# A one-core trunk kernel: stick-breaking attention outputs computed channel-major by column tiles, their norm moved

## The reference, cut to what matters

```python
z = einsum("bqhd,bkhd->bhqk", q_i, k_p) * scale
w = exp(where(past, z + suffix, -inf))     # suffix: sums of log sigmoid(-z)
outs.append(einsum("bhqk,bkhd->bqhd", w, v_p))
...
sb_o = rms_norm(stick_breaking_attention(q, k, v), sb_gain)   # over each head's 64 channels
```

## Time and profile before

| | us |
|---|---|
| median of 3 runs | 1591.11 |
| lowest, highest | 1590.86, 1613.55 |
| profiled execution | 1608.1 |
| its span | 1606.4 |

### The profile page before, as it was taken

The page is one execution under the profiler, slowest core; times in us unless marked ns, Lnnn a source line. Parts: engine busy times, 40 slices in busy tenths (PEclk is TensorE's granted clock), DMA queues, the critical chain, the costliest instruction groups (busy, mean ns, idle before and its releaser), DMA issues.

```text
span 1606.4 us, 22550 instructions
## 1 busy us (share of the span) xinstructions
PE 1535.4 (96%) x8129; PEld 1294.0 (81%) x8129; DVE 700.9 (44%) x1283; ACT 479.2 (30%) x1089; POOL 529.0 (33%) x478
## 2 busy tenths in 40 slices
PE   5999999999987999999999999999999999999997
PEld 4778888888867888888887888888888888888885
DVE  5105546455443567666224143334333443344337
ACT  5223444454342334443344211111111111111114
POOL 3112332333233446654342323323323332332331
PEclk8999999999995899989999999999999999999999
DMA  5112222332232122221521211111111111111112
GB/s 171 41 52 68 84 67 81 115 91 79 65 108 77 48 79 64 63 79 52 195 80 50 69 53 52 40 52 52 46 45 52 40 51 52 52 39 52 52 40 104
DMA packets 144602, 110.61 MB, mean 69 GB/s; under 512 B 5568, under 2 KB 132112, under 8 KB 144528
## 3 DMA queue, kind: packets, MB, share of 16 engines
q1 hardware_dynamic: 144384, 109.11, 22.6%
q10 hardware_dynamic: 144, 0.52, 0.1%
HBM read 88.63 MB, written 20.99 MB: 68 GB/s over the span
## 4 chain that ended last, share of the span: by engine, by line
PE 91%; DVE 6%; issue 1%; ACT 1%; POOL 1%; DMA 0%; DVEq 0%; SPq 0%; POOLq 0%
PE banks L1738 10%; PE banks L1740 10%; PE banks L1739 10%; PE banks L259 9%; PE banks L261 9%; PE banks L260 9%; PE banks L1777 5%; PE banks L1778 5%; PE banks L1776 5%; PE banks L947 3%; PE banks L961 3%; PE banks L644 2%; PE banks L996 2%; PE banks L954 1%; PE banks L621 1%; DVE area L1841 1%
## 5 line engine op out<-in xcount | busy, mean ns | idle before, releaser
L251 POOL TENSOR_TENSOR w_l<-w_raw,w_h 128x1024 fp32r<-128x1024 f32 x113 | 274.7, 2431 | 645.1 <-ACT w_h L1785 345.9
L1738 PE MATMUL banks<-act_h,w_h 128*128 128x512 f32 x704 | 275.0, 391 | 2.4 <-DVE act_l L310 2.4
L1740 PE MATMUL banks<-act_h,w_l 128*128 128x512 f32 x704 | 274.5, 390 | 0.0
L1739 PE MATMUL banks<-act_l,w_h 128*128 128x512 f32 x704 | 274.5, 390 | 0.0
L259 PE MATMUL banks<-act_h,w_h 128*128 128x512 f32 x624 | 251.1, 402 | 8.0 <-POOL w_l L251 5.5
L261 PE MATMUL banks<-act_h,w_l 128*128 128x512 f32 x624 | 245.2, 393 | 0.0
L260 PE MATMUL banks<-act_l,w_h 128*128 128x512 f32 x624 | 244.6, 392 | 0.0
L1841 DVE TENSOR_TENSOR area<-area,banks 128x512 f32<-128x512 f32 x352 | 237.4, 687 | 0.0
L1835 DVE TENSOR_TENSOR area<-banks,area 128x512 f32<-128x512 f32 x44 | 30.4, 692 | 443.3 <-PE banks L1740 442.5
L1738 PEld LDWEIGHTS banks<-act_h,w_h 128*128 128x128 f32 x704 | 132.5, 188 | 30.0 <-DVE act_l L310 2.6
L1740 PEld LDWEIGHTS banks<-act_h,w_l 128*128 128x128 f32 x704 | 132.6, 188 | 27.6
(11 more groups left out here) (192 smaller groups left out, 2040.3 us busy)
## 6 DMA issues: line engine op xcount, KB each, us to landing
w_raw<-in_w_in SPq DMA_DIRECT2D x31, 512.0 KB, 4.0
w_raw<-in_w_gate SPq DMA_DIRECT2D x22, 512.0 KB, 3.8
w_raw<-in_w_up SPq DMA_DIRECT2D x22, 512.0 KB, 3.8
w_raw<-in_w_down SPq DMA_DIRECT2D x22, 512.0 KB, 3.5
area<-in_x SPq DMA_DIRECT2D x8, 1024.0 KB, 9.2
projected_tm<-area SPq DMA_DIRECT2D x32, 256.0 KB, 2.9
w_raw<-in_w_out SPq DMA_DIRECT2D x16, 512.0 KB, 3.6
projected_cm<-area SPq DMA_DIRECT2D x20, 256.0 KB, 2.2
```

The source lines that it names most:

```text
L251: e.tensor_tensor(w_l[:, b], w_raw[:, b], w_h[:, b].bitcast(F32), ALU.subtract).then_inc(sems["wl_ready"], 1)
L1738: e.matmul(dst, w_h[:, b, k], act_h[:, k, cols], start=(k == 0), stop=False)
L1739: e.matmul(dst, w_h[:, b, k], act_l[:, k, cols], start=False, stop=False)
L1740: mm = e.matmul(dst, w_l[:, b, k], act_h[:, k, cols], start=False, stop=(k == KT - 1))
```

## The change

- **Values.** `weigh` swaps the operands: the 64 channels of v are stationary, the 128 tokens of `wt` move, so that the output has channels on the partitions. Head 0 goes to PSUM partitions 0-63, head 1 to 64-127 of the same columns: two column tiles of the PE array. Both units of a pair are weighed together, in odd slots, the heads in turns.
- **Store.** The output goes to its own DRAM tensor `attended`, [2, 128 channels, 1024 tokens]; `projected_tm` loses its last 256 columns. The squares on ACT and their waits are gone.
- **Norm.** In the mixer's step t = -1 four pieces (head pair x 512 tokens) are loaded into `gate`, squared on ACT, summed per head over the partitions by a PE matmul with a block matrix of ones, Ln and Exp on ACT, times gain on DVE, split into `act_h` (ACT) and `act_l` (DVE). SP issues piece i's load after piece i - 1's product (`so_done`).
- **Mixer.** `final_sb` is gone, `mix` has 768 channels, the second `mix_turn` has 2 transposes instead of 4 and waits for `fin_hg` alone, the first for `fin_dn`. `gates` and the first output product wait for the pieces. Constants grow by one memset and two selects on POOL.

```diff
-    TM = SB_AT + SBW
+    TM = SB_AT
...
+    sb_dram = nc.dram_tensor("attended", [2, P, T], F32, kind="Internal").ap()
...
+            m = head_ones[:, :].rearrange("p (b r) -> p b r", r=64)
+            select(m, ALU.is_ge, 0, [[-64, 2], [0, 64]], 1, 0.0)
+            select(m, ALU.is_ge, 63, [[64, 2], [0, 64]], -1, 0.0)
...
-                e.dma_start(tm_dram[q * P:(q + 1) * P, SB_AT + hp * P:SB_AT + (hp + 1) * P],
-                            o_stage[:, u % 2]).then_inc(sems[f"o_stored{u % 2}"], 16)
+                e.dma_start(sb_dram[hp, :, q * P:(q + 1) * P], o_stage[:, u % 2]).then_inc(sems[f"o_stored{u % 2}"], 16)
...
-                reach(e, "wt_ready", k + 1)
-                if hh == 0 and at == 0:
+                e.wait_ge(sems["wt_ready"], k + 2)
+                if at == 0:
                     reach(e, "o_evac", u)
                 for j in range(n // P):
                     m = NT - 1 - q + at // P + j
-                    mm = e.matmul(Ov[:, u % 2, hh, :], wt[:, k % 2, j * P:(j + 1) * P],
-                                  v_tm[:, m, hp * P + hh * SBD:hp * P + (hh + 1) * SBD],
-                                  start=(hh == 0 and at == 0 and j == 0), stop=(at + (j + 1) * P == (q + 1) * P), skip_group_check=True)
-                mm.then_inc(sems["av_done"], 1)
+                    for hh in range(2):
+                        mm = e.matmul(O[hh * SBD:(hh + 1) * SBD, u % 2 * P:(u % 2 + 1) * P],
+                                      v_tm[:, m, hp * P + hh * SBD:hp * P + (hh + 1) * SBD], wt[:, (k + hh) % 2, j * P:(j + 1) * P],
+                                      start=(at == 0 and j == 0), stop=(at + (j + 1) * P == (q + 1) * P), skip_group_check=True)
+                        if j == n // P - 1:
+                            mm.then_inc(sems["av_done"], 1)
...
-                if 2 <= k < NH + 2:
-                    weigh(k - 2)
+                if 3 <= k < NH + 2 and k % 2 == 1:
+                    weigh(k - 3)
...
-            def out_squares(k):
-                hp, q = UNITS[k][:2]
-                u = unit_of(k)
-                reach(e, "o_evac", u + 1)
-                reach(e, "o_sq", u)
-                for hh in range(2):
-                    ins = e.activation(junk_o[:, hh, :], o_stage[:, u % 2, hh * SBD:(hh + 1) * SBD], ACT.Square,
-                                       accum_out=ssq_sb[:, q, 2 * hp + hh:2 * hp + hh + 1])
-                ins.then_inc(sems["o_sq"], 1)
...
+        def piece(i):
+            return i // 2, slice(i % 2 * HALF, (i % 2 + 1) * HALF)
+
+        def attended_sync(e, i):
+            hp, cols = piece(i)
+            reach(e, "so_done", i)
+            e.dma_start(gate[:, 0:HALF], sb_dram[hp, :, cols]).then_inc(sems["so_loaded"], 16)
+
+        def attended_sums(e, i):
+            e.wait_ge(sems["so_sq"], i + 1)
+            reach(e, "so_ln", i)
+            e.matmul(bank(4), head_ones[:, :], junk_dn[:, :, :], start=True, stop=True).then_inc(sems["so_sum"], 1)
+
+        def attended_squares(e, i):
+            e.wait_ge(sems["so_loaded"], 16 * (i + 1))
+            reach(e, "so_sum", i)
+            e.activation(junk_dn[:, :, :], heads(gate[:, 0:HALF]), ACT.Square).then_inc(sems["so_sq"], 1)
+
+        def attended_length(e, i):
+            e.wait_ge(sems["so_sum"], i + 1)
+            reach(e, "so_low", i)
+            e.activation(mix[:, 0:HALF], bank(4), ACT.Ln, scale=1.0 / SBD, bias=eps_col[:, 0:1]).then_inc(sems["so_ln"], 1)
+            e.wait_ge(sems["so_ln"], i + 1)
+            e.activation(mix[:, 0:HALF], mix[:, 0:HALF], ACT.Exp, scale=-0.5).then_inc(sems["so_r"], 1)
+
+        def attended_high(e, i):
+            hp, cols = piece(i)
+            e.wait_ge(sems["so_done"], i + 1)
+            e.activation(act_h[:, hp, cols], mix[:, 0:HALF], ACT.Copy).then_inc(sems["so_high"], 1)
+
+        def attended_done(e, i):
+            e.wait_ge(sems["so_r"], i + 1)
+            e.wait_ge(sems["gain_col_loaded"], 32)
+            e.scalar_tensor_tensor(out=mix[:, 0:HALF], in0=gate[:, 0:HALF], scalar=gain_col[:, 0:1], in1=mix[:, 0:HALF],
+                                   op0=ALU.mult, op1=ALU.mult).then_inc(sems["so_done"], 1)
+
+        def attended_low(e, i):
+            hp, cols = piece(i)
+            e.wait_ge(sems["so_high"], i + 1)
+            e.wait_ge(sems["so_done"], i + 1)
+            e.tensor_tensor(act_l[:, hp, cols], mix[:, 0:HALF], act_h[:, hp, cols].bitcast(F32), ALU.subtract).then_inc(sems["so_low"], 1)
...
+                if t == -1:
+                    for i in range(4):
+                        attended_sync(e, i)
...
-                    e.wait_ge(sems["fin_sb"], c + 1)
+                    e.wait_ge(sems["fin_dn"], c + 1)
                     reach(e, "hs_new", min(c + 1, NT - 1))
                     reach(e, "act_low", 2 * c - 1)
                 else:
                     e.wait_ge(sems["fin_hg"], c + 1)
-                e.wait_ge(sems["fin_dn"], c + 1)
-                for k in range(4):
+                for k in range(4 - 2 * n):
...
                 if live(u):
                     update(u, 2)
+                if t == -1:
+                    attended_sums(e, 0)
                 if t == NT:
...
                 if live(u):
                     inverse(u, 1)
+                if t == -1:
+                    attended_squares(e, 0)
+                if live(u):
                     from_start(u)
                 if live(u, NT - 1):
...
                 if live(u):
                     inverse(u, 2)
+                if t == -1:
+                    attended_length(e, 0)
+                    attended_high(e, 0)
+                    attended_squares(e, 1)
+                if live(u):
                     spans(u, 0, 3)
                 if live(s):
...
-            def final_sb(c):
-                e.wait_ge(sems["pb_loaded"], 16 * (c + 1))
-                reach(e, "mt_done", 2 * c - 1)
-                final(c, SBH, pb[:, SB_AT - 2 * DNW:], r_sb[:, c, :], SBD, 0, gain_row[:, 0:SBW], "fin_sb")
...
                 if live(u):
                     pack(u, 3)
+                if t == -1:
+                    attended_done(e, 0)
+                    attended_low(e, 0)
                 if live(v):
                     apart(v)
...
                 if live(t):
-                    final_sb(t)
                     final_dn(t)
...
                 reach(e, "fin_dn", c)
+                e.wait_ge(sems["so_done"], 4)
...
             if i == 0:
+                e.wait_ge(sems["so_low"], 4)
                 e.wait_ge(sems["act_low"], NT)
```

More of the change, by code:

```diff
@@ L126, in trunk_program @@
         ab_tm = sb("ab_tm", [P, NT, 2 * DNH])
-        small = {n: sb(n, [P, NT, DNH]) for n in ("g_all", "beta", "gc", "rest", "whole", "eg", "rk", "d_all", "vbs", "neg_d", "eps_q", "r_sb")}
-        g_all, beta, gc, rest, whole, eg, rk, d_all, vbs, neg_d, eps_q, r_sb = small.values()
-        ssq_qk, ssq_sb = sb("ssq_qk", [P, 2, NT, DNH]), sb("ssq_sb", [P, NT, SBH])
+        small = {n: sb(n, [P, NT, DNH]) for n in ("g_all", "beta", "gc", "rest", "whole", "eg", "rk", "d_all", "vbs", "neg_d", "eps_q")}
+        g_all, beta, gc, rest, whole, eg, rk, d_all, vbs, neg_d, eps_q = small.values()
+        ssq_qk = sb("ssq_qk", [P, 2, NT, DNH])
+        head_ones, gain_col = sb("head_ones", [P, P]), sb("gain_col", [P, 1])
         gc_rows = sb("gc_rows", [NT * DNH, P])
@@ L761, in mix_act @@
                     key_squares(k - 4)
-                if 4 <= k < NH + 4 and ENDS[k - 4]:
-                    out_squares(k - 4)
         def mixed_to_dram(e):
@@ L1208, in high @@
                 e.wait_ge(sems["mt_done"], 2 * c + n + 1)
-                act(act_h[:, 4 * n:4 * n + 4, c * P:(c + 1) * P], heads(bank(6 + n)), ACT.Copy, "act_high")
+                first, last = (2, 6) if n == 0 else (6, 8)
+                act(act_h[:, first:last, c * P:(c + 1) * P], heads(bank(6 + n)[:, 0:(last - first) * P]), ACT.Copy, "act_high")
             def from_start(c):
@@ L1382, in low @@
                 e.wait_ge(sems["act_high"], 2 * c + n + 1)
-                tt(act_l[:, 4 * n:4 * n + 4, c * P:(c + 1) * P], heads(bank(6 + n)),
-                   act_h[:, 4 * n:4 * n + 4, c * P:(c + 1) * P].bitcast(F32), ALU.subtract, "act_low")
+                first, last = (2, 6) if n == 0 else (6, 8)
+                tt(act_l[:, first:last, c * P:(c + 1) * P], heads(bank(6 + n)[:, 0:(last - first) * P]),
+                   act_h[:, first:last, c * P:(c + 1) * P].bitcast(F32), ALU.subtract, "act_low")
             def new_state(c):
@@ L1476, in step @@
                     pack(u, 4)
+                if t == -1:
+                    attended_done(e, 1)
+                    attended_low(e, 1)
                 if live(t):
@@ L1498, in step @@
                     pack(u, 6)
+                if t == -1:
+                    attended_done(e, 3)
+                    attended_low(e, 3)
+                if live(u):
                     for lv in range(1, LEVELS):
@@ L1882, in _ @@
```

(4 more changed lines are left out.)

56 lines of the change are left out of this document (34 added, 22 removed).

## The result

| | before | after |
|---|---|---|
| median | 1603.49 us, 20 runs | 1615.98 us, 20 runs |
| lowest, highest | 1589.90, 1613.55 | 1611.53, 1627.46 |
| profiled execution, its span | 1608.1, 1606.4 | 1620.33, 1618.5 |

A forecast was written before the change was run, and what follows sets the result against it. It took PE to bound the lead and an engine-to-engine chain to bound step t = -1. Terms -10.1 + 27.4 - 5.8 = +11.5 us on 1591.1 gave 1602.6 us, own range 1595 to 1610, chance 0.58; wider range 1587 to 1620.

The forecast's parts named there:

- What bounds the kernel: PE full in the lead, so its instructions count; in step t = -1 a chain from engine to engine, nobody full.
- Part 1: Lead, weights times values: column tiles side by side at 0.056 us a pass, 32.0 us falling to 21.9, -10.1 us.
- New waits: Lead, within the values term: weighing pairs in odd slots and freeing the wt buffer later add no waiting, 0.
- Part 2: Step t = -1, norm and split: four pieces stop the inverse's rounds, +10.1, +13.9 and 3.4, +27.4 us in all.
- Rival 3: Step t = -1: the pieces fit into idle time, only some 4 us show; -12, 1579 us, chance 0.06.
- Part 3: Steady steps: PE's 0.59 us wait goes seven times, 4.1, and two transposes per chunk, 1.7; -5.8 us.
- I take 0: Steady steps: half-clock spells could fall otherwise when steps are shorter, between 0 and -8 us more; taken as 0.
- the base: Whole kernel: 1591.1 us, median of three runs, to which +11.5 was added, though the profiled execution took 1608.1.
- Rival 1 and 2: Lead: column tiles in series, +27.7, 1619 us, chance 0.18; weights and stream not overlapping either, +41.5, 1633, chance 0.08.
- Rival 4: Step t = -1 stop smaller, and the steps' slow-clock spells gained: -5, 1586 us, chance 0.10.

The follow-up runs named there:

- in SBUF and spread: Changed kernel with attended blocks kept on chip, each piece's logarithm, exponential and product one round ahead of its high part: 1589.55 us, ratio 0.9948.
- run 22: Not a run's number: the words are "a highest run 22 us above the other two", of the unchanged kernel's three runs, 1590.9, 1591.1 and 1613.6 us.

## Why the prediction was wrong, point by point

- **What bounds the kernel, and which view says so: right.** In the lead a PE instruction saved was time saved; in t = -1 the busy sums said nothing and the chain everything.
- **Part 1, -10.1 us: right**, measured -10.5 in the profiles, and the whole of it in the time with the tiles alone. The mechanism and the price of a pass were right, 0.056 us forecast and 0.055 measured; that the total came within 0.4 us is partly luck. A pass was 0.112 us before, not 0.101 (I had divided a group's 0.81 by eight, without looking at the smaller groups), a group's own cost now is 0.15 us, not 0.24, so that the rows fell by 11.6 us; and of "New waits: ... Nothing" one of 0.69 us came. The Trainium skill's rule (TensorEngine Tiling (Array Packing), When to Use Tiling: swap and 2x column tiling for 64 columns on the right side) has the right sign; by the trace it is 2x on the spacing of the passes and 1.6x on the rows as a whole (31.1 to 19.4 us), with the tiles in turns.
- **Part 2, +27.4 us: right**, measured +26.0. The first load went out at 490.26 (501.2 less the lead's 10.1 is 491.1), pack(3) at 496.96 (predicted 497.4 on the same footing), the period was 10.45 to 10.58 (predicted 10.7), pack(6) at 528.50 (529.5). Rival 3, "the pieces fit into the idle time", was wrong for this kernel, and right for the work itself: in SBUF and spread it costs nothing.
- **Part 3, -5.8 us: the profile agrees, the time does not show it.** PE's wait of 0.59 us went, and a step is 0.67 shorter (0.81 predicted); the 0.22 of the two transposes was taken back by the new wait of 0.29, so that the -5.9 of the profile against -5.8 has 1.2 us of luck in where the spells fell. But the kernel without `final_sb` alone is at 1.0005, and the changed kernel without pieces is no faster than the tiles alone. Three terms as measured in means of runs, from the ratios over some 1600 us, are some -14 for the tiles, nothing for the steps and +31 for the pieces (1.0114 less 0.9918), which makes +17, the ratio's +18 within its error; each is uncertain by 6 to 7. "The half-clock spells in these steps could fall otherwise ... I take 0" is where it rests: a spell is worth 3.1 us, more than four steps' gain, and where spells fall differs from one execution to the next of the same text.
- **The step that failed: the base, and with it the granted clock put at nothing.** "What moves does not hang on that: median 1591.1 + 11.5" took the sum, made in an execution of 1608.1 us, over to a median of three that was 17 us lower. 20 runs of the kernel before have a median of 1603.49, 12.4 above the base, and that is most of the 13.4 us by which 1602.6 missed 1615.98. In the experiments every execution of the kernel before at 1590 to 1592 us has a mean clock of 0.977 or more, so 1590.9 and 1591.1 were most likely executions in which the clock stayed high, and between 1590.6 us at 0.98 and 1607.8 at 0.967 the kernel before moves without any change to it. I had the warning in hand, a highest run 22 us above the other two and a profile 17 us above the median.
- **The same step in the change itself: "I take 0" for the half-clock spells.** The ratio stands for 14 to 22 us more, and +11.5 lies outside; run again, the changed kernel gave 15 to 30. What moves does hang on the clock: the changed kernel has 64 us of mixer at a mean of 0.56 where there were 38.6, and (64.4 - 38.6) x 0.44 / 1618 is 0.007 of mean clock less. That explains a part only: the kernel before reaches 0.982, and of the 26 executions of the changed one none went above 0.968. So it was partly luck that 1603.49 + 11.5 = 1615.0 meets the median within a microsecond, and the profile's 1619.6 met 1620.33: in means of the 20 runs the difference is 17.0 us (1600.9 to 1617.9).
- **Rival 1 and 2** (tiles in series) fell by the group of 1.03 us, though rival 1's time, 1619, came nearer to the measured 1615.98 than the forecast did: it stood on the same base, and the two errors nearly met. **Rival 4** (spells gained) fell too: the clock was lost, not gained.

What stays open: why the shorter steps give nothing back in the time, and why the changed kernel never has the high clocks. The runs show spells moving to later steps and the tail, in profiles of single executions; they don't show what decides where they fall.

## What to carry to other kernels

Judge a small change against many runs of the kernel before, and take the base of a forecast from an execution like the profiled one: where the time of one text moves by 1% with the granted clock, a median of three is no base. A chain that goes round the engines once per link has idle time only for work that nobody in the round waits for: bring the data early, put each operation a round ahead of its use, and it is free; put a load, a square and a sum between two links and each costs its whole latency. Where PE waits in short pieces at half clock, products that nobody reads can be worth more than they cost (6.5 us for 80 of them here), but count them so that they don't outlast the wait at half clock. Price an array pass from groups of several sizes: the slope is the pass, what is left over is the group.

## What the runs showed of the hardware

- Two column tiles of 64 run side by side. Passes of one tile start 0.11 us apart, those of the two tiles some 6 ns. 16 fp32 passes of 128 columns take 1.03 us in turns and 1.52 us with eight of one tile ahead of eight of the other, where only four of each overlap; 8 passes take 0.59 and 0.60 us.
- Filling PE's waits raised the granted clock in a stretch from 0.56 to 0.81, PE's own rows from 1.97 to 1.10 us. The Trainium skill (TensorE: Matmul & The Clock Gate, HAM oscillation — how this bites in real kernels) describes waits for a DMA that bring the clock down again and again, and advises another loop order. The trace agrees that PE's waiting goes with the low clock, here with waits of 0.5 to 0.8 us for DVE and ACT, and shows that a filler does as well.
- Fillers of 0.6 us ahead of two packs of each step, where from step 1 on there was little to fill (one wait of 0.29 us), left spells of 3.4 to 10.2 us in the profile.
- The kernel before, unchanged, takes 1590 to 1592 us at a mean clock of 0.977 to 0.982 and 1597 to 1613 at 0.966 to 0.975, on one and the same chip.
